# Turning attention probabilities ahead of the outputs of the pair in front, in the first block of a two-block forward pass

## The chip, the cores and the metric

The kernel runs on one core of one Trainium2 chip. Its time is the device time of one execution in microseconds (us). TensorE (PE) does matmuls and transposes, VectorE (DVE) and ScalarE (ACT) do everything that works on whole tiles, GpSimd (POOL) adds up norms, and SyncE (SP) issues the weight loads.

## The reference, cut to what matters

Two transformer blocks run one after the other on 256 tokens of width 1024, in float32. The first block has two layers (`DEPTH = 2`), and takes 256 context tokens along. Each of its layers mixes tokens in three ways (attention, an mLSTM and a pooling mixer), projects the result (`w_out`) and has a SwiGLU. The change touches the attention of these two layers alone:

```python
def block_attention(q, k, v):          # 8 query heads, 2 key heads, head size 64
    ...
    def one_block(qi):                 # 128 queries
        s = jnp.einsum('bqhgd,bkhd->bhgqk', qi, k, preferred_element_type=F32) * scale
        p = jax.nn.softmax(s, -1).astype(v.dtype)
        return jnp.einsum('bhgqk,bkhd->bqhgd', p, v)

# hybrid_layer
    att_l = block_attention(q_l, jnp.concatenate([k_l, k_c], 1), jnp.concatenate([v_l, v_c], 1))
    ...
    xl = xl + g1_l * (jnp.concatenate([att_l, ml_l, pool_l], -1) @ w_out)
    if with_ctx_out:                   # layer 0 only
        att_c = block_attention(q_c, k_c, v_c)
```

A block of 128 latent queries of one head meets 512 keys, a block of 128 context queries meets 256.

## The kernel before, in words

Every engine has its own instruction stream, written out by hand, and waits on semaphores for the others. The attention of a layer is split into units: one head of one block of 128 queries. Two units, one for each key head, make a pair. Layer 0 has 32 units in 16 pairs: 8 pairs with 512 keys, then 8 with 256. Layer 1 has 16 units in 8 pairs, all with 512 keys. I write S(i) for the scores of pair i, T(x) for the turning (transposing) of unit x, and O(i) for the outputs of pair i; pair i is the units 2i and 2i+1.

- PE (`pe_attention`), at step i: S(i) into PSUM (line 1328, semaphore `at_s`), then O(i-2), the product of values and turned probabilities (line 1342, `at_o`), then T(2i-2) and T(2i-1) (line 1353, `at_t`). O(i-2) waits until both turned units of its pair have been copied out of PSUM (`at_pt`). T(x) waits until unit x's probabilities are normalised (`at_p`), and until the PSUM bank that it shares with unit x-2 has been copied out (`at_pt`). At step 1, the readout of the mLSTM is turned as well (line 1607).
- DVE (`dve_attention`), at step j: the row maximum of unit j (line 1394, needs S), its scaling (1395, `at_max`), the reciprocal of the sum of unit j-1 (1400), the normalising of unit j-1 (1402, `at_p`), and at every second step the low half of an output (1411, `at_out`). At steps 3 and 5, pieces of the mLSTM readout are in it (1807, 1814), and at step 8 the split of a weight tile (580).
- ACT (`act_attention`), at step j: the exponentials of unit j (1370, `at_exp`), the copy of turned unit j-2 out of PSUM (1378, `at_pt`), and at every second step the high half of the output of a pair three in front (1383). At step 8, it also has the split of a weight tile (571).

A weight tile of the projections is split into a high and a low part: ACT writes the high one (571), DVE the rest (580). The projection behind the attention (`pe_residual`, lines 600 to 602 for each of its three products) needs the attention's last output. SP loads weights into a ring of buffers (line 553), two of its transfers start while the two attentions run; none is issued from PE.

Of the kernel before, what the change touches and what calls it, by code (L numbers as in the profile page):

```python
# [12 lines left out]
P = 128  # L13
# [419 lines left out]
def build(nc, dram, out):  # L433
    ctx = ExitStack()
    with ctx:
# [3 lines left out]
        def sem(name):  # L439
            return ctx.enter_context(nc.semaphore(name))  # L440
# [58 lines left out]
        ps = ctx.enter_context(nc.psum_tensor("ps", [P, 8, 512], F32))  # L499

        def K(name):
            at, n = CONST_AT[name]
            return const[:, at:at + n]
# [788 lines left out]
        def dve_keys(dve, layer):  # L1292
# [6 lines left out]
        at_s, at_max, at_exp, at_p, at_t, at_pt, at_o, at_high, at_out = (  # L1299
            sem(f"at_{x}") for x in ("scores", "max", "exp", "probs", "turned", "probsT", "o", "high", "out"))  # L1300

        def attention_units(layer):


            turns = [(2, 3), (0, 1)] if layer < DEPTH - 1 else [(2, 3)]
            return [(qt, j, b, (2 if qt < 2 else 4) * P) for turn in turns for j in range(4) for qt in turn for b in range(2)]
# [3 lines left out]
        def score_bank(x):  # L1310
            return 2 + x % 4

        def pe_attention(pe, layer):


            units, base = attention_units(layer), AT_BASE[layer]
            n = len(units) // 2
            pe.wait_ge(qk_k, layer + 1)
            pe.wait_ge(ml_h, 4 * layer + 4)
            for i in range(n + 2):  # L1320
                if i == 1:
                    pe.wait_ge(pl_low, layer + 1)
                if i < n:
                    if i >= 2:
                        pe.wait_ge(at_exp, base + 2 * i - 2)
                    for x in (2 * i, 2 * i + 1):
                        qt, j, b, nk = units[x]
                        pe.matmul(ps[:, score_bank(x), 0:nk], proj[64 * b:64 * b + 64, AQ + j, qt * P:(qt + 1) * P],
                                  proj[64 * b:64 * b + 64, AK, 0:nk], start=True, stop=True).then_inc(at_s, 1)
                if i == 1:  # L1330
                    pe_readout(pe, layer)
                if i >= 2:
                    p = i - 2
                    nk = units[2 * p][3]
                    pe.wait_ge(at_pt, base + 2 * p + 2)
                    if p == 0:
                        pe.wait_ge(ml_mixed, layer + 1)
                    if p >= 2:
                        pe.wait_ge(at_out, base // 2 + p - 1)
                    for s in range(nk // P):  # L1340
                        for b in range(2):
                            mm = pe.matmul(ps[64 * b:64 * b + 64, p % 2, 0:P], tm[:, s, AV + 64 * b:AV + 64 * b + 64],  # L1342
                                           probsT[(2 * p + b) % 4][:, s * P:(s + 1) * P], start=(s == 0), stop=(s == nk // P - 1),
                                           skip_group_check=True)
                            if s == nk // P - 1:
                                mm.then_inc(at_o, 1)
                if 1 <= i <= n:
                    for x in (2 * i - 2, 2 * i - 1):
                        pe.wait_ge(at_p, base + x + 1)
                        if x >= 2:  # L1350
                            pe.wait_ge(at_pt, base + x - 1)
                        for s in range(units[x][3] // P):
                            mm = pe.transpose(ps[:, 6 + x % 2, s * P:(s + 1) * P], probs[x % 4][:, s * P:(s + 1) * P], K("ident"))
                        mm.then_inc(at_t, 1)
            pe.wait_ge(at_out, base // 2 + n)

        def act_attention(act, layer):
# [132 lines left out]
        probs = [ebuf[:, b, d] for b in range(2) for d in range(2)]  # L1490
# [20 lines left out]
        def ml_tiles(layer):  # L1511
            return range(0, 4) if layer < DEPTH - 1 else range(2, 4)
# [90 lines left out]
        def pe_readout(pe, layer):  # L1603
            pe.wait_ge(ml_hn, layer + 1)
            for tt in ml_tiles(layer):
                for f in range(2):
                    mm = pe.transpose(ps[:, f, tt * P:(tt + 1) * P],
                                      hsum[:, tt, 2 * f:2 * f + 2, :].rearrange("p h v -> p (h v)"), K("ident"))
            mm.then_inc(ml_hT, 1)
# [1231 lines left out]
        @block.tensor  # L2841
        def _(pe):
            pe_ada(pe)
            for layer in range(DEPTH):
                c0, n = unit_tokens(layer, False)
                pe_project(pe, layer)
                pe_mlstm(pe, layer)
                pe_attention(pe, layer)
                pe_residual(pe, f"out{layer}", mix, c0, n, KT, norm=2 * layer + 1, order=OUT_ORDER)
                pe_ffn(pe, layer, 2 * layer + 1, 2 * layer + 2)  # L2850
            pe_ffn(pe, 2, 5, 6)
            pe_qkv(pe)
            pe_second(pe)
            pe_rwkv(pe)
            pe_merge(pe)
            pe_residual(pe, "w_o", merged, 0, T, KT, norm=7)
            pe_ffn(pe, 3, 7, 8)
# [220 lines left out]
```

## Time and profile before

| | us |
|---|---|
| runs (three) | 2003.0, 2010.8, 2010.97; median 2010.8 |
| the profiled execution, its own time | 2009.54 |
| its span, first to last instruction | 2007.7 |
| attention of layer 0, S(0) to the projection | 62.7 (222.76 to 285.48) |
| attention of layer 1, S(0) to the projection | 40.7 (875.52 to 916.21) |

The profile gives, for one execution, when each instruction started and how long it took, and for each idle stretch what ended it. Its page says that PE is busy for 1865.1 us of the span, DVE for 1134.5 and ACT for 757.2, and that the mean granted TensorE clock is 0.968 of full speed. Starts are in microseconds from the first instruction. A matmul's end is modelled, so its length holds some time in which the next one is already under way: the distance between two starts is what one costs its successor.

### The profile page before, as it was taken

To read this page: it belongs to the slowest core of one execution; us is meant where nothing else is said; L and a number is where in the kernel's file an instruction comes from. 1 tells how busy PE (TensorE), PEld (TensorE's weight loads), DVE (VectorE), ACT (ScalarE), POOL (GpSimd) and SP (SyncE) were. 2 spreads that over 40 slices of the span, in tenths; PEclk is the share of its full clock that TensorE was granted. 3 is DMA by queue.
4 is the path that set the end of the run, shared out by engine and by line. 5 is a ranking of instruction groups with operands and counts; after the bars stand their busy time and mean duration, and the time that the engine had idled before them with its cause. 6 is when DMAs were issued, how large, how long until landed. Compare 5 with 4: busy or idle time off the path is not lost.

```text
span 2007.7 us, 34066 instructions
## 1 busy us (share of the span) xinstructions
PE 1865.1 (93%) x14848; PEld 1632.5 (81%) x14848; DVE 1134.5 (57%) x1692; ACT 757.2 (38%) x1054; POOL 307.7 (15%) x270
## 2 busy tenths in 40 slices
PE   6999888999999979988999999999998999889998
PEld 3777555877888768857999999989987777789997
DVE  2644565554353338566555576556765666566654
ACT  3432563221122225355333443343454333344332
POOL 1011001999080010100000100002001111000000
PEclk8999999999999988898999999999999999999999
DMA  8154112565353222203555555544340111255552
GB/s 339 64 191 183 68 43 84 182 211 173 121 186 123 85 74 72 76 22 105 185 177 184 200 189 177 176 144 165 128 158 23 44 44 44 77 173 174 188 173 80
DMA packets 39605, 266.20 MB, mean 133 GB/s; under 512 B 4384, under 2 KB 4512, under 8 KB 11168
## 3 DMA queue, kind: packets, MB, share of 16 engines
q1 hardware_dynamic: 34560, 244.10, 35.2%
q0 software_dynamic: 4608, 16.78, 2.7%
q8 instruction: 117, 1.92, 0.4%
q10 hardware_dynamic: 288, 3.15, 0.4%
q14 instruction: 32, 0.26, 0.0%
HBM read 262.96 MB, written 1.05 MB: 131 GB/s over the span
## 4 chain that ended last, share of the span: by engine, by line
PE 78%; DVE 9%; POOL 5%; ACT 5%; issue 2%; DMA 1%; SPq 0%; ACTq 0%; DVEq 0%; POOLq 0%
PE ps L600 19%; PE ps L601 18%; PE ps L602 18%; PE ps L2751 3%; POOL work L1015 2%; DVE W L580 2%; PE ps L926 1%; PE ps L606 1%; PE ps L1555 1%; POOL work L1016 1%; PE ps L608 1%; PE ps L607 1%; PE ps L1342 1%; DMA ring<-w_ada_dram 1%; PE ps L2297 1%
## 5 line engine op out<-in xcount | busy, mean ns | idle before, releaser
L580 DVE TENSOR_TENSOR W<-ring,W 128x2048 fp32r<-128x2048 f32 (+2 forms) x194 | 439.5, 2267 | 260.6 <-ACT W L571 260.3
L571 ACT ACTIVATE W<-ring 128x2048 fp32r<-128x2048 f32 (+2 forms) x194 | 359.0, 1853 | 136.0 <-PE ps L602 129.0
L600 PE MATMUL ps<-h_lat,W 128*128 128x256 f32 x1056 | 301.9, 286 | 4.0 <-DVE h_lat L747 4.0
L601 PE MATMUL ps<-h_lat,W 128*128 128x256 f32 x1056 | 300.0, 284 | 0.0
L602 PE MATMUL ps<-h_lat,W 128*128 128x256 f32 x1056 | 299.9, 284 | 0.0
L600 PEld LDWEIGHTS ps<-h_lat,W 128*128 128x128 f32 x1056 | 203.6, 193 | 5.5 <-issue 4.6
L601 PEld LDWEIGHTS ps<-h_lat,W 128*128 128x128 f32 x1056 | 204.0, 193 | 0.3 <-issue 0.2
L602 PEld LDWEIGHTS ps<-h_lat,W 128*128 128x128 f32 x1056 | 203.9, 193 | 0.0
L699 POOL TENSOR_TENSOR work<-work 128x512 f32<-128x512 f32 (+1 forms) x48 | 48.7, 1014 | 997.4 <-ACT work L681 806.9
L600 PE MATMUL ps<-hidden_lat,W 128*128 128x256 f32 x528 | 150.4, 285 | 6.3 <-DVE hidden_lat L912 6.3
L601 PE MATMUL ps<-hidden_lat,W 128*128 128x256 f32 x528 | 150.2, 284 | 0.0
L602 PE MATMUL ps<-hidden_lat,W 128*128 128x256 f32 x528 | 150.1, 284 | 0.0
L909 DVE TENSOR_TENSOR work<-work,ps 128x256 f32<-128x256 f32 (+1 forms) x88 | 42.9, 488 | 189.3 <-ACT work L884 189.2
L600 PE MATMUL ps<-h_both,W 128*128 128x512 f32 x352 | 140.6, 399 | 9.0 <-DVE h_both L747 9.0
L601 PE MATMUL ps<-h_both,W 128*128 128x512 f32 x352 | 137.7, 391 | 0.0
L602 PE MATMUL ps<-h_both,W 128*128 128x512 f32 x352 | 137.6, 391 | 0.0
L884 ACT ACTIVATE work<-ps 128x512 f32<-128x512 f32 (+1 forms) x44 | 21.6, 491 | 267.7 <-PE ps L602 267.7
L600 PEld LDWEIGHTS ps<-hidden_lat,W 128*128 128x128 f32 x528 | 102.1, 193 | 6.9 <-DVE hidden_lat L912 6.9
L602 PEld LDWEIGHTS ps<-hidden_lat,W 128*128 128x128 f32 x528 | 102.1, 193 | 0.0
L601 PEld LDWEIGHTS ps<-hidden_lat,W 128*128 128x128 f32 x528 | 102.0, 193 | 0.0
L681 ACT ACTIVATE work<-xT 128x256 f32<-128x256 f32 (+1 forms) x64 | 31.5, 497 | 173.6 <-DVE xT L645 115.0
L600 PE MATMUL ps<-h_mix,W 128*128 128x256 f32 x312 | 93.3, 299 | 3.9 <-DVE h_mix L745 3.9
(387 smaller groups left out, 4207.0 us busy)
## 6 DMA issues: line engine op xcount, KB each, us to landing
ring<-w_up_dram SPq DMA_DIRECT2D x88, 1024.0 KB, 5.0
ring<-w_down_dram SPq DMA_DIRECT2D x43, 1024.0 KB, 4.9
ring<-w_ada_dram SPq DMA_DIRECT2D x32, 1024.0 KB, 6.0
work<-w_ada_dram POOLq DMA_DIRECT2D x32, 512.0 KB, 4.3
ring<-w_rkv_dram SPq DMA_DIRECT2D x13, 1024.0 KB, 5.0
ring<-w_fm_dram SPq DMA_DIRECT2D x10, 1024.0 KB, 4.9
ring<-w_out_dram SPq DMA_DIRECT2D x8, 1024.0 KB, 4.9
ring<-w_gates_dram SPq DMA_DIRECT2D x8, 1024.0 KB, 4.9
```

What stands on the lines that cost most here:

```text
L571: act.activation(slots[SLOT[s]][:, 0, 0:cols], ring[:, u % RING, 0:cols], ACT.Copy).then_inc(w_high, 1)
L580: dve.tensor_tensor(slots[SLOT[s]][:, 1, 0:cols], ring[:, u % RING, 0:cols], slots[SLOT[s]][:, 0, 0:cols], ALU.subtract).then_inc(w_low, 1)
L600: pe.matmul(o, slots[SLOT[s]][:, 0, at:at + cols], high, start=first, stop=False)
L601: pe.matmul(o, slots[SLOT[s]][:, 0, at:at + cols], low, start=False, stop=False)
L602: return pe.matmul(o, slots[SLOT[s]][:, 1, at:at + cols], high, start=False, stop=final)
L606: pe.matmul(o, high, slots[SLOT[s]][:, 0, at:at + cols], start=first, stop=False)
L681: ins = act.activation(square[:, at, 0:n], xT[:, m, c0:c0 + n], ACT.Square, scale=1.0 / 32)
L699: pool.tensor_tensor(square[:, 0, 0:n], square[:, 0, 0:n], square[:, square_at(m), 0:n], ALU.add).then_inc(norm_add, 1)
L884: act.activation(stage_buf[:, i % 2, 0:n], gate, ACT.Silu).then_inc(act_emptied, 1)
L909: dve.tensor_tensor(t, t, up_banks(g, n)[1], ALU.mult).then_inc(dve_emptied, 1)
L1015: plink(pool.tensor_tensor(half, half, c, ALU.mult))
L2751: mm = pe.matmul(ps[:, 3, m * T:(m + 1) * T], ring[:, u % RING, x * P:(x + 1) * P], h2[:, k, :], start=(k == 0), stop=(k == KT - 1))
```

## The change

In the PE stream of `pe_attention` alone, the block that turns T(2i-2) and T(2i-1) is moved ahead of the block that makes O(i-2). The order at step i was S(i), O(i-2), T(2i-2), T(2i-1); it becomes S(i), T(2i-2), T(2i-1), O(i-2). Every wait stays with the instruction that it belonged to. The streams of ACT, DVE, POOL and SP are the same, and so is the arithmetic. Both layers of the first block run through this code.

```diff
                 if i == 1:
                     pe_readout(pe, layer)
+                if 1 <= i <= n:
+                    for x in (2 * i - 2, 2 * i - 1):
+                        pe.wait_ge(at_p, base + x + 1)
+                        if x >= 2:
+                            pe.wait_ge(at_pt, base + x - 1)
+                        for s in range(units[x][3] // P):
+                            mm = pe.transpose(ps[:, 6 + x % 2, s * P:(s + 1) * P], probs[x % 4][:, s * P:(s + 1) * P], K("ident"))
+                        mm.then_inc(at_t, 1)
                 if i >= 2:
                     p = i - 2
                     nk = units[2 * p][3]
...
                             if s == nk // P - 1:
                                 mm.then_inc(at_o, 1)
-                if 1 <= i <= n:
-                    for x in (2 * i - 2, 2 * i - 1):
-                        pe.wait_ge(at_p, base + x + 1)
-                        if x >= 2:
-                            pe.wait_ge(at_pt, base + x - 1)
-                        for s in range(units[x][3] // P):
-                            mm = pe.transpose(ps[:, 6 + x % 2, s * P:(s + 1) * P], probs[x % 4][:, s * P:(s + 1) * P], K("ident"))
-                        mm.then_inc(at_t, 1)
             pe.wait_ge(at_out, base // 2 + n)
```

## Rows read from the trace of the kernel before

**Rows 1.** Page, part 4: the chain that ended last, shares of the span by engine.

```profile
PE 78%; DVE 9%; POOL 5%; ACT 5%; issue 2%; DMA 1%; SPq 0%; ACTq 0%; DVEq 0%; POOLq 0%
```

**Rows 2.** Timeline, one 512-key step: start, length, engine, line, operation, count, [idle before].

```profile
250.86 1.13 PE L1328 MATMUL ps<-work 64*128 64x512 f32 x4
...
252.02 0.69 DVE L1394 TENSOR_REDUCE work<-ps 128x1 f32<-128x512 f32 x1 [0.40 <-PE ps L1328]
252.59 1.09 PE L1342 MATMUL ps<-work 128*64 128x128 f32 x16 [0.61 <-ACT work L1378]
...
253.06 0.49 DVE L1402 TENSOR_SCALAR work<-work 128x512 f32<-128x512 f32 x1
...
253.62 1.09 PE L1353 MATMUL ps<-const,work 128*128 128x128 f32 x8
...
254.31 0.60 ACT L1378 ACTIVATE work<-ps 128x512 f32<-128x512 f32 x1 [0.45 <-PE ps L1353]
...
254.64 1.13 PE L1328 MATMUL ps<-work 64*128 64x512 f32 x4
...
254.96 0.78 ACT L1370 ACTIVATE work<-ps,work 128x512 f32<-128x512 f32 x1
...
255.72 0.61 ACT L1378 ACTIVATE work<-ps 128x512 f32<-128x512 f32 x1
...
256.38 1.09 PE L1342 MATMUL ps<-work 128*64 128x128 f32 x16 [0.61 <-ACT work L1378]
```

**Rows 3.** Timeline, one 256-key step.

```profile
265.34 0.70 PE L1328 MATMUL ps<-work 64*128 64x256 f32 x4
...
266.07 0.42 DVE L1394 TENSOR_REDUCE work<-ps 128x1 f32<-128x256 f32 x1
...
266.65 0.66 PE L1342 MATMUL ps<-work 128*64 128x128 f32 x8 [0.61 <-ACT work L1378]
...
266.85 0.35 DVE L1402 TENSOR_SCALAR work<-work 128x256 f32<-128x256 f32 x1
...
267.24 0.65 PE L1353 MATMUL ps<-const,work 128*128 128x128 f32 x4
...
267.71 0.38 ACT L1378 ACTIVATE work<-ps 128x256 f32<-128x256 f32 x1 [0.28 <-PE ps L1353]
...
267.83 0.70 PE L1328 MATMUL ps<-work 64*128 64x256 f32 x4
```

**Rows 4.** Timeline around the split of a weight tile, layer 0.

```profile
245.03 0.49 DVE L1402 TENSOR_SCALAR work<-work 128x512 f32<-128x512 f32 x1
...
245.58 0.76 PE L1353 MATMUL ps<-const,work 128*128 128x128 f32 x4 [3.89 <-DVE work L1402]
...
246.27 2.08 PE L1328 MATMUL ps<-work 64*128 64x512 f32 x4
```

**Rows 5.** Timeline, ends of the attention of layer 0 and of layer 1.

```profile
277.78 0.70 PE L1328 MATMUL ps<-work 64*128 64x256 f32 x4
...
281.49 0.35 DVE L1402 TENSOR_SCALAR work<-work 128x256 f32<-128x256 f32 x1
...
283.67 1.12 PE L1342 MATMUL ps<-work 128*64 128x128 f32 x8 [0.84 <-DVE mix L1411]
...
905.84 1.13 PE L1328 MATMUL ps<-work 64*128 64x512 f32 x4
...
911.05 0.49 DVE L1402 TENSOR_SCALAR work<-work 128x512 f32<-128x512 f32 x1
...
914.38 1.09 PE L1342 MATMUL ps<-work 128*64 128x128 f32 x16 [0.91 <-ACT work L1378]
```

**Rows 6.** Windows: stretch, its us, busy us of each engine, granted clock, DMA share, GB/s.

```profile
277.78:285.48 7.70, 4.32 (x37) 2.72 (x36) 4.35 (x17) 4.94 (x18) 0.00 (x0) 0.87 0.00 1
285.50:290.40 4.90, 4.90 (x12) 3.84 (x13) 3.46 (x2) 3.20 (x2) 0.00 (x0) 0.50 0.19 25
290.40:295.30 4.90, 4.90 (x23) 4.04 (x22) 1.91 (x3) 0.63 (x1) 0.00 (x0) 1.00 0.86 348
```

## Prediction, made before the change was run

> **What bounds the kernel now.** The chain that ended last comes first: 78% of it is PE [rows 1], so whatever delays PE on this chain is paid in full. The two attentions last 62.7 and 40.7 us, 103 of 2008, so what the change can move is small. Within them the question is what closes one step of the loop, and the timeline of one step answers it.
>
> With 512 keys, one step takes 3.78 us from S to S (250.86 to 254.64). PE waits in one place: O starts at 252.59 after 0.61 idle, released by ACT's copy L1378 [rows 2]. Follow that loop: O start to T start 1.03 (252.59 to 253.62); T start to ACT's first copy 0.69 (to 254.31, and ACT had idled 0.45 for it); then the small high half and the exponentials, 0.65 to 254.96; exponentials to the second copy 0.76 (255.72); its 0.61 and a 0.05 hand-over to the next O at 256.38. Sum: 1.03 + 0.69 + 0.65 + 0.76 + 0.66 = 3.79, the step. So O, T and ACT bound it, and DVE's work lies beside O. With 256 keys the step is 2.49 (265.34 to 267.83), with O again behind 0.61 of idle released by the same copy [rows 3].
>
> **The change, part by part.** Nothing is added or taken away: O and T keep their counts and lengths. Two things happen.
>
> Removed: O (1.03) no longer stands between S and T, so ACT's copy of the first unit can come earlier and the loop above is cut. That much looks like a gain.
>
> Moved in front: T(2i-1) needs the probabilities of unit 2i-1, and DVE normalises these only behind the maximum of unit 2i, which needs S(i). In the trace this cannot be overtaken: the maximum starts at 252.02 after 0.40 idle, released by S, 1.16 after S's start; then 1.04 over scaling and reciprocal to the normalising (253.06), and 0.49 for it [rows 2]. Before, O filled PE during this. After, PE has only T(2i-2), whose probabilities are there, and then stands in front of T(2i-1), with O(i-2) and S(i+1) queued behind the wait. DVE and ACT wait for that S(i+1) in turn. The new loop, S to S, with 512 keys:
>
> - S to maximum 1.16, maximum to normalising 1.04, normalising 0.49 and hand-over 0.06 (245.03 + 0.49 to T at 245.58) [rows 2, 4]: T(2i-1) starts 2.75 behind S.
> - T(2i-1), four transposes and the change to the next group: 0.59 (267.24 to 267.83) [rows 3].
> - O: 1.03 [rows 2]. Sum 2.75 + 0.59 + 1.03 = 4.37, against 3.79: **0.58 longer**.
>
> With 256 keys: S to maximum 0.73, maximum to normalising 0.78 (266.07 to 266.85), 0.35 and 0.05, so T(2i-1) at 1.91. Its two transposes: four take 0.59 and eight take 1.02, so one takes 0.11, and two take 0.37. O, eight matmuls, 0.59 (266.65 to 267.24). Sum 2.87 against 2.49: **0.38 longer** [rows 2, 3].
>
> The maximum's 0.73 with 256 keys could be less, as DVE was not idle there; it is bounded below by S's own length, 0.70 [rows 3]. The hand-over I bound by 0.02 and 0.08. Neither moves the sum by over 0.5 us in all. That O behind T could start quicker, its weights loaded during the wait, could give back at most what O shows as change of group beyond its matmuls (1.03 - 8 x 0.11 = 0.15) in some 18 steps, 2.7 us at the most; below nothing I see no reason. I take no such gain, since a wait ahead of O in the trace leaves its 1.03 as it is [rows 2].
>
> Now the count. **Layer 0**: by the first weight split S has moved little. By walking the order forward with the terms above, S(3) comes 0.95 later (the first outputs, 1.03, lay under DVE's readout before, and now follow it) and S(4) 0.4 more; but the split stalls everyone (PE idle 3.89 until T(7) at 245.58) [rows 4] and takes most of that. What gets past is the later T(5), 0.33, which ACT's stream carries into the split, and O(2), 1.03, which ran before the stall and now stands behind it: S(5) comes 1.35 later. Three steps of 0.58 follow (S(5) to S(8)): 3.1 in all. The two steps at the change to 256 keys have terms of both kinds and give -0.1 and +0.2. Five steps of 0.38 (S(10) to S(15)): 5.1. ****Its end** gains: the last T no longer stands behind an O that waits. Before, unit 31's probabilities were ready 4.06 behind S(15) (281.49 + 0.35 - 277.78); 0.28 of that was ACT waiting for a T that now comes early, so T(31) starts at 4.06 - 0.28 + 0.05 = 3.8. Its copy begins 0.47 later and takes 0.38, 0.05 to hand over: last O at 4.7, where it was 5.9 (283.67) [rows 3, 5]; 1.1 is given back. Sum +4.0 us.: T(31) needs only its probabilities, 3.74 behind S(15) by ACT's and DVE's rows, and the last O follows at 3.74 + 0.47 + 0.44 + 0.05 = 4.70. Before it was 5.85; so 1.1 is given back. Sum +4.0 us.
>
> **Layer 1**: S(5) 1.6 later by the same steps, two steps of 0.58 to S(7), 2.8. At its end, unit 15's probabilities were ready 5.70 behind S(7) (911.05 + 0.49 - 905.84); without ACT's wait of 0.45 for T, T(15) starts at 5.3, and 0.59 and 1.03 later comes the last O, at 6.9, against 8.54 (905.84 to 914.38) [rows 2, 5]: 1.7 back. Sum +1.1 us.
>
> Both: **+5.1 us**. Behind either attention the projection waits for the last output, so the 5.1 goes through in full. No DMA is issued by PE; SP's load during the split moves by less than 1 us. Made against the profiled execution's own time, 2009.54 + 5.1 = 2014.6; that execution lies 1.3 under the median of the runs, 2010.8, from which the same sum gives 2015.9; between the two I forecast 2015.
>
> **The clock.** At the end of layer 0 PE is busy 4.32 of 7.70 us, and afterwards the projection starts at granted clock 0.50, the 1.2 GHz level: 12 matmuls in 4.90 us, where the next 4.90 us at full clock hold 23 [rows 6]. That costs 11/23 x 4.9 = 2.3 us. A shorter end may save that, and a loop with 0.6 us more idle may bring such a fall elsewhere. The Trainium skill's page "TensorE: Matmul & The Clock Gate", section "What's actually happening", says that the throttled state is the default and activity lifts it. It speaks against this change, which makes PE idler in each step; the trace agrees as far as its falls follow idle stretches.
>
> **The rivals.**
>
> *The gate takes the loop (slower by over 0.5%).* S took 2.08 in place of 1.13 in the one step at 1.2 GHz [rows 4]. In the new loop S, T(2i-1) and O are all in the chain: some 0.95 + 0.45 + 0.9 = 2.3 more in each 512-key step, 1.3 in each 256-key step. It decides from the point where the new idle in a step (PE busy about 3.2 of 4.37, where it was 3.2 of 3.78) makes the clock fall; in all 10 and 8 steps that is 33 us, 2048; in a quarter of them 8 us, 2023. For it: the fall at the end of layer 0, with busy 4.32 of 7.70 = 0.56. Against: busy stays near 0.7.
>
> *The end gains the clock.* The sum, less the 2.3: 2012.
>
> *ACT's loop was all (faster).* If T(2i-1) found its probabilities ready, the step would fall to DVE's own work, about 3.15 with 512 keys (3.78 less DVE's 0.40 idle and the wait for ACT ahead of its low half, some 0.2), 0.6 less in 12 steps and next to nothing with 256 keys, and the ends' 2.8: -10 us, 2000. For it: PE's only steady wait is ACT's. Against: the maximum of 2i stands ahead of the normalising of 2i-1 in DVE's stream.
>
> *It doesn't do what it says.* If PE could let O pass the waiting T, nothing would be lost, 2010. By the same page, section "Step-by-step: what each phase is for", matmuls stay in program order. The trace shows the same: T and S never start while O waits [rows 2].
>
> **How the numbers follow.** Forecast 0.66; the end gains the clock 0.14; nothing changes 0.06; faster 0.05; gate 0.09. The three runs of before spread over 8 us (2003.0 to 2010.97), which no row explains, and widens each case: the range goes from 2006 to 2022, which leaves out most of the faster case and of the gate. A difference of 0.5% (10 us, under 2000.7 or over 2020.9) is about what can be told from none: faster 0.04 (half of its case, and scatter), slower 0.13 (the gate and scatter of the forecast), no difference 0.83.
>
> **What would show it.** Right: S to S 4.37 and 2.87 in steady steps; T(2i-1) alone behind idle time released by DVE L1402, some 1.0 us per 512-key step; O without idle ahead of it; ACT's copy no longer waiting for T(2i-2); last O to the projection as before, at 6.9 behind layer 1's last S. Wrong: steps at or under 3.78 with idle still released by ACT; a granted clock of 0.50 within the steady steps; or the attentions' lengths as forecast (66.7 and 41.8 us) and the total not.

## The result

| | before | changed |
|---|---|---|
| median of 20 runs each | 2010.32 us (2003.0 to 2015.17) | 2017.86 us (2011.6 to 2025.18) |
| ratio, 95% interval | 1 | 1.004, 1.0029 to 1.005 |
| span of the profiled execution | 2007.7 | 2016.8 |
| attention of layer 0, S(0) to the projection | 62.72 | 67.81 |
| attention of layer 1 | 40.68 | 42.55 |
| the 512-key step, S to S | 3.78 | 4.36 |
| the 256-key step | 2.49 | 2.88 |

The change makes the kernel slower by 0.4%, 6 to 10 us. In the two profiles, the attentions account for 5.1 + 1.9 = 7.0 us of a span that is 9.0 longer. The ratio isn't the quotient of the two medians, and the two can be some us apart where the times lie in groups; below, each difference says which it is taken from. One execution of the kernel before, in the last group of runs, took 2648.13 us at a granted clock of 0.65, and is left out.

The timeline of the changed kernel, a 512-key step (start, length, engine, line; [idle before it <- what ended it]); it answers to [rows 2]. T is line 1338 now, O is line 1350.

```profile
254.64 1.13 PE L1328 MATMUL ps<-work 64*128 64x512 f32 x4
...
255.70 0.66 PE L1338 MATMUL ps<-const,work 128*128 128x128 f32 x4
255.80 0.69 DVE L1394 TENSOR_REDUCE work<-ps 128x1 f32<-128x512 f32 x1 [1.19 <-PE ps L1328]
...
256.85 0.49 DVE L1402 TENSOR_SCALAR work<-work 128x512 f32<-128x512 f32 x1
...
257.39 0.66 PE L1338 MATMUL ps<-const,work 128*128 128x128 f32 x4 [1.03 <-DVE work L1402]
...
257.55 0.58 ACT L1378 ACTIVATE work<-ps 128x512 f32<-128x512 f32 x1
...
257.98 1.09 PE L1350 MATMUL ps<-work 128*64 128x128 f32 x16
...
259.00 0.70 PE L1328 MATMUL ps<-work 64*128 64x512 f32 x2
```

Read it as a ring. S starts at 254.64; the maximum of unit 2i follows 1.16 later, and DVE had been idle 1.19 for it, where that was 0.40. The normalising of unit 2i-1 starts 1.05 behind the maximum, and 0.54 after its start T(2i-1) begins: PE idled 1.03 for it. O and the next S have no wait of their own left, they only come 0.59 and 1.02 behind. Sum 1.16 + 1.05 + 0.54 + 0.59 + 1.02 = 4.36. The 256-key step, which answers to [rows 3], is the same ring with shorter pieces:

```profile
273.21 0.70 PE L1328 MATMUL ps<-work 64*128 64x256 f32 x4
...
274.72 0.35 DVE L1402 TENSOR_SCALAR work<-work 128x256 f32<-128x256 f32 x1
...
275.13 0.44 PE L1338 MATMUL ps<-const,work 128*128 128x128 f32 x2 [0.85 <-DVE work L1402]
...
275.49 0.66 PE L1350 MATMUL ps<-work 128*64 128x128 f32 x8
...
276.08 0.49 PE L1328 MATMUL ps<-work 64*128 64x256 f32 x2
```

PE's waits in the attention of layer 0, summed by who ended them (total, times, longest). The same view of the kernel before has 8.9 us in 13 waits of O for ACT's copy, and 5.0 in 3 of T for DVE. One wait has taken the place of the other, and is larger.

```profile
PE ps L1338 <- DVE work L1402: 17.5, 15, 4.5
PE ps L1328 <- DVE mix L1461: 1.8, 1, 1.8
```

The weight split, which answers to [rows 4]:

```profile
247.04 0.66 PE L1338 MATMUL ps<-const,work 128*128 128x128 f32 x4 [4.47 <-DVE work L1402]
247.63 1.96 PE L1350 MATMUL ps<-work 128*64 128x128 f32 x16
249.51 1.90 PE L1328 MATMUL ps<-work 64*128 64x512 f32 x4
```

Here O, 1.09 long elsewhere, is 1.96, and S 1.90 in place of 1.13. The windows view (us, busy of each engine, granted clock) shows the clock at 0.51, the 1.2 GHz level, in just this stretch, behind 4.47 us of idle PE. The second and third row answer to [rows 6]: the end of layer 0's attention, 7.00 us where it was 7.70, and the first 4.9 us of the projection.

```profile
247.63:251.10 3.47, 3.47 (x21) 2.06 (x20) 0.96 (x4) 1.59 (x5) 0.00 (x0) 0.51 0.60 248
284.71:291.71 7.00, 5.03 (x38) 3.10 (x36) 3.85 (x16) 4.37 (x16) 0.00 (x0) 0.78 0.01 4
291.70:296.60 4.90, 4.89 (x14) 3.90 (x15) 3.44 (x2) 3.23 (x2) 0.00 (x0) 0.62 0.12 13
```

### The profile page after: what moved, and what is told of

Same layout as the page of the kernel before. It is cut to its first block, busy times and chain, and to the rows that moved or that the text cites. A ratio compares the mean times of both kernels' runs of the same rounds, so it can differ in the third digit from the quotient of the medians.

```text
span 2016.8 us, 34066 instructions
## 1 busy us (share of the span) xinstructions
PE 1873.8 (93%) x14848; PEld 1637.0 (81%) x14848; DVE 1133.5 (56%) x1692; ACT 756.4 (38%) x1054; POOL 307.4 (15%) x270
## 3 DMA queue, kind: packets, MB, share of 16 engines
HBM read 262.96 MB, written 1.05 MB: 131 GB/s over the span
## 4 chain that ended last, share of the span: by engine, by line
PE 80%; DVE 9%; POOL 4%; ACT 3%; issue 2%; DMA 1%; SPq 0%; DVEq 0%; ACTq 0%; POOLq 0%
PE ps L600 19%; PE ps L601 19%; PE ps L602 19%; PE ps L2751 3%; POOL work L1015 2%; PE ps L926 1%; DVE W L580 1%; PE ps L1555 1%; PE ps L606 1%; PE ps L607 1%; PE ps L608 1%; PE ps L1350 1%; POOL work L1016 1%; DMA ring<-w_ada_dram 1%; PE ps L2297 1%
```

## The experiments

The theory at this point: T(2i-1) needs a normalising that stands behind a maximum that needs S(i), and O, once beside that chain, now stands in it, ahead of S(i+1). Rivals: clock falls in any place, the move as such, or the wait of T(2i-1) alone. All ratios below are to the kernel before on the same chip. The comments in the cuts of code are added here.

### One layer alone

Layer 0 alone, against the changed kernel; layer 1 alone has the two numbers exchanged.

```diff
-                if 1 <= i <= n:
+                if layer == 0 and 1 <= i <= n:     # the turns ahead of O(i-2)
...
+                if layer == 1 and 1 <= i <= n:     # the turns behind O(i-2)
```

> The new order in layer 0 alone, the old one in layer 1. Theory (the step is closed by S, DVE's normalising, T(2i-1), O): layer 0 shows what the changed kernel shows, S to S 4.36 and 2.88, attention about 67.5 us, where it was 62.7, and layer 1 stays at 40.7; the time is 4 to 5 us over before (ratio 1.0020 to 1.0025). Rival (the measured loss is mostly clock falls that the changed order brings anywhere): the ratio need not split by layers, and could be all of 1.004 or none.

> The new order in layer 1 alone. Theory: attention of layer 1 about 42.5 us where it was 40.7, layer 0 at 62.7; 1 to 2 us over before (ratio 1.0005 to 1.001), so that this and the kernel with layer 0 alone add up to the whole change. Rival: 3 us or more over before with layer 1's attention still at 42.5, the rest in clock falls elsewhere.

Layer 0 alone: 1.0028 (1.0012 to 1.0044), attentions 67.85 and 41.23 us, steps 4.36 and 2.88. Layer 1 alone: 1.002 (1.0006 to 1.0035), attentions 62.53 and 42.44. Each layer shows the lengths of the whole change where the new order is, and nearly those of before where it isn't (41.23 against 40.68: its step with the split was 8.35 long, where 7.89 was). The ratios add up to 1.0048, against 1.004. Layer 1's 4 us by the ratio (2.9 by the medians) are above the 1 to 2 that were expected, and are what the rival named (3 or more with that attention still at 42.5); the interval, 1 to 7 us, excludes neither. So the attentions' lengths split as the theory says; the time of so small a part can't decide between the two.

### The first turn alone ahead of O

T(2i-2) goes ahead of O(i-2), T(2i-1) stays behind it. The cut is against the kernel before.

```diff
+                if 1 <= i <= n:
+                    for x in (2 * i - 2,):
...
                 if i >= 2:
                     p = i - 2
...
                 if 1 <= i <= n:
-                    for x in (2 * i - 2, 2 * i - 1):
+                    for x in (2 * i - 1,):
```

> Half of the change: T(2i-2) goes ahead of O(i-2), T(2i-1) stays behind it. Theory: only the turn that has to wait for DVE's normalising does the harm, and the other one, ahead, lets ACT copy it earlier. O then fills PE while DVE normalises. Walking the order forward with the terms of the trace, a 512-key step takes 3.33 (3.78 before) and a 256-key step 2.35 (2.49); layer 0 ends 4.1 and layer 1 2.3 us earlier: 6 us under before (ratio 0.997). Rival (any move of turns ahead of outputs costs, since outputs then stand behind a copy or a bank that is not free): steps at or over 3.78 and the time at or over before.

Measured 0.9957 (0.9941 to 0.9973), median 1999.72 us: faster than before. The timeline of one of its 512-key steps (T(2i-2) is line 1338, O 1350, T(2i-1) 1361) has PE without a wait that the view shows:

```profile
251.75 1.13 PE L1328 MATMUL ps<-work 64*128 64x512 f32 x4
252.81 0.66 PE L1338 MATMUL ps<-const,work 128*128 128x128 f32 x4
253.39 1.09 PE L1350 MATMUL ps<-work 128*64 128x128 f32 x16
254.50 0.65 PE L1361 MATMUL ps<-const,work 128*128 128x128 f32 x4
255.08 1.13 PE L1328 MATMUL ps<-work 64*128 64x512 f32 x4
```

3.33 from S to S, as walked, and 2.29 with 256 keys (2.35 walked). T(2i-1) starts 2.75 behind S here too (251.75 to 254.50): that is DVE's distance, unchanged, but O lies beside it. The rival that any turn ahead of O costs has fallen. The attentions are 4.2 us shorter than before (59.67 and 39.56), less than the 4.1 + 2.3 expected: around the split, S(4) to S(6) lasts 8.26 + 5.70 in layer 0, where it was 7.91 + 4.59. The time gained is 10.6 us by the medians and 8.6 by the ratio (5 to 12), so more than the attentions show, while the 6 expected aren't excluded.

### The scores ahead of O

The whole change, and S(i+1) goes between T(2i-1) and O(i-2). The cut is against the changed kernel.

```diff
-                if i < n:
-                    if i >= 2:
-                        pe.wait_ge(at_exp, base + 2 * i - 2)
+                if i < 2:
...
+                if 1 <= i < n - 1:                  # behind the turns, ahead of O(i-2)
+                    pe.wait_ge(at_exp, base + 2 * i)
+                    for x in (2 * i + 2, 2 * i + 3):
```

> The whole change, and S(i+1) is issued behind T(2i-1) but ahead of O(i-2). Theory: what made the changed kernel slow is that S(i+1), and with it DVE, stands behind O; with O out of that loop the step is S, DVE's normalising, T(2i-1): 4.37 less 1.03, 3.33, and 2.35 with 256 keys. 7.5 us under before (ratio 0.9963), although T(2i-1) still waits for DVE. Rival (the wait of T(2i-1) for DVE is itself the loss, wherever O stands): steps near 4.36 stay, and the time is some 5 us over before.

Measured 0.9977 (0.9966 to 0.9988), attentions 59.18 and 38.28 us, steps 3.33 and 2.29. The step is 1.03 shorter than in the changed kernel, the length of O. A 512-key step (S is line 1342, O 1354, T 1336):

```profile
257.88 1.13 PE L1342 MATMUL ps<-work 64*128 64x512 f32 x4
258.94 1.09 PE L1354 MATMUL ps<-work 128*64 128x128 f32 x16
259.97 1.32 PE L1336 MATMUL ps<-const,work 128*128 128x128 f32 x8
261.22 1.13 PE L1342 MATMUL ps<-work 64*128 64x512 f32 x4
```

T(2i-1) loads its weights at 260.63, again 2.75 behind S, but O lies in this distance, and PE has no wait that the view shows. With 256 keys 0.26 us of wait are left in each step. The view of PE's waits in layer 0 still has 10 for DVE, but 8.0 of its 9.3 us lie at the start, the split and the end:

```profile
PE ps L1336 <- DVE work L1406: 9.3, 10, 4.6
```

So the rival that steps stay near 4.36 wherever O stands has fallen: what costs is that S(i+1), which feeds DVE, stands behind O, which stands behind the wait. Not shown is a step in which the wait stays and costs nothing. Written out, the order here is S(i+1), O(i-2), T(2i), T(2i+1): the order of the kernel before, with the outputs one pair further back, whose inputs have long been copied. The 0.61 us of idle in front of O [rows 2] are gone, which is why it beats before; it isn't the changed order with a repair.

The time is 4.6 us under before by the ratio (2 to 7) and 7.2 by the medians, where 7.5 were expected. The profiled execution, 2006.42, lies 3.3 over the median; its first attention begins at 227.99 where the others begin near 222.7, behind a clock fall at 158 us, in code that is the same in all kernels.

### The normalising ahead of the maximum

The changed kernel, and DVE does the normalising of unit 2i-1 before the maximum of unit 2i.

```diff
+                if 1 <= i <= n and i % 2 == 0:      # ahead of the maximum of unit i
+                    x = i - 1
+                    dve.wait_ge(at_exp, base + x + 1)
...
-                if 1 <= i <= n:
+                if 1 <= i <= n and i % 2 == 1:
```

> The changed kernel, and DVE normalises unit 2i-1 ahead of the maximum of unit 2i, at every second step. Theory: T(2i-1) waited because this normalising stood behind a maximum that needs S(i). Taking it out of the way frees T(2i-1) from S(i); the step then closes through ACT's exponentials: walked forward, 3.86 with 512 keys (4.36 in the changed kernel) and 2.83 with 256 (2.88), 2.1 us under the changed kernel, 3 over before. Rival (T(2i-1) waits for something else, such as the exponentials alone): steps stay 4.36, and the time too.

Measured 1.0021 (1.0008 to 1.0033), 4.2 us over before by the ratio where 3 were expected. The 512-key steps are 3.70 to 3.88 and the 256-key steps 2.84 to 2.85, as walked; the attentions 66.33 and 41.24 us, 2.8 less than in the changed kernel. PE's wait ahead of T(2i-1) falls from 1.03 to 0.38 and 0.56 (timeline, T line 1338):

```profile
255.41 0.66 PE L1338 MATMUL ps<-const,work 128*128 128x128 f32 x4 [0.38 <-DVE work L1396]
...
259.30 0.66 PE L1338 MATMUL ps<-const,work 128*128 128x128 f32 x4 [0.56 <-DVE work L1396]
```

So the maximum that needs S(i) is in the ring. With 512 keys nearly all of the 0.58 comes back (steps 0.48 to 0.66 shorter), with 256 keys only 0.03 of 0.39: DVE now waits for ACT's exponentials ahead of this normalising (0.47 and 0.24 idle), which close the next ring. The step with the split is longer than in the changed kernel, 9.53 and 9.71 for 8.66 and 9.14.

### Extra turns during the split

36 transposes of the identity into the bank that T(7) overwrites, between the two waits of T(7). Put into the changed kernel and into the one before. The two waits change places ahead of every turn, which is a second difference.

```diff
                     for x in (2 * i - 2, 2 * i - 1):
-                        pe.wait_ge(at_p, base + x + 1)
                         if x >= 2:
                             pe.wait_ge(at_pt, base + x - 1)
+                        if x == 7:
+                            for _ in range(36):
+                                pe.transpose(ps[:, 7, 0:P], K("ident"), K("ident"))
+                        pe.wait_ge(at_p, base + x + 1)
```

> The changed kernel, and while PE waits for the weight split (4.47 us idle ahead of T(7)) it turns the identity 36 times into bank 7, which T(7) overwrites: about 3.9 us of extra matmuls in idle time. Theory: what the changed kernel lost over the walk (1.9 us in the two attentions) is the low clock behind this wait, which now meets O as well as S. Without it, S(4) to S(5) and S(5) to S(6) go from 8.66 and 5.13 to 7.8 and 4.36 in layer 0, from 9.14 and 5.10 to 7.8 and 4.36 in layer 1; the attentions last about 66.2 and 40.5, and the time is some 3.7 us under the changed kernel, 4 over before. Rival (the split's wait itself is longer in the new order): the steps stay over 8.5.

> The kernel before with the same 36 extra turns in the same wait. Theory: here only S and what follows in one step ran at the low clock, S(5) to S(6) 4.59 and 4.84 where a step is 3.78, so 1.9 us come back: ratio 0.999. Against this kernel the changed one with extra turns is 5.1 us slower, the walk's sum without any clock term. Rival: the low clock costs both orders the same, so that the two with extra turns differ by the same 6.9 us (in the two attentions) as the two without.

Changed kernel with extra turns: 1.0006 (0.9993 to 1.0019). Its timeline at the split:

```profile
242.78 4.09 PE L1338 MATMUL ps<-const 128*128 128x128 f32 x36
247.35 0.66 PE L1341 MATMUL ps<-const,work 128*128 128x128 f32 x4 [0.48 <-DVE work L1405]
247.94 1.09 PE L1353 MATMUL ps<-work 128*64 128x128 f32 x16
```

O is back at 1.09. S(4) to S(5) and S(5) to S(6) are 7.74 and 4.42 in layer 0 (8.66 and 5.13 in the changed kernel), 7.75 and 4.42 in layer 1 (9.14 and 5.10). The rival, a longer wait for the split, has fallen: it was the low clock behind it. Layer 1's attention lasts 40.74, as expected (40.5). Layer 0's, 67.23, is 1 over its 66.2: a clock fall came earlier, at 235 us, behind 1.98 us of idle PE, and steps S(2) to S(4) were 5.56 and 5.37 long. A plain miss is the steady step, 4.42 and 2.94, 0.06 more each; the exchanged waits are the only difference in these steps.

The kernel before with extra turns: 0.9983 (0.9971 to 0.9994), S(4) to S(5) and S(5) to S(6) 7.75 and 3.70 in layer 0, attentions 61.27 and 39.55, 2.6 us less where 1.9 were expected; 0.5 of it is the end of layer 0, which had no clock fall here. Its steady steps stay at 3.78 and 2.49, so the exchanged waits cost nothing where PE has idle time in front of O.

The rival was that the two orders with extra turns still differ by 6.9 us in the attentions. They do differ by 7.2, so the sum doesn't speak for the theory. Layer by layer: in layer 1, where no clock fall disturbs either, they differ by 40.74 - 39.55 = 1.19 us, against 1.1 walked and 1.87 without extra turns. In layer 0 they differ by 5.96; the fall at 235 us, which stands ahead of the extra turns, made two steps 1.3 longer, and the exchanged waits cost some 0.7, which leaves 3.9 against 4.0 walked. This is a subtraction, and no run shows layer 0 of the changed kernel at full clock throughout. Going by the ratios, each good to some 2.5 us either way, the two kernels differ by 4.6 us, which can't part 5.1 from 6.9.

### A version that beats both, and repeats

The first turn ahead of O, both turns ahead in the last step, and the extra turns. The cut is against the kernel with the first turn alone ahead, and leaves the extra turns out.

```diff
+                if i == n and 1 <= i <= n:          # T(2i-1) ahead of O(i-2), last step only
...
-                if 1 <= i <= n:
+                if i < n and 1 <= i <= n:
```

> A version that should beat both: T(2i-2) ahead of O(i-2), T(2i-1) behind it, except in the last step, where both go ahead, and the 36 extra turns in the wait for the split. Theory: steps of 3.33 and 2.29 as with the first turn alone; the ends 0.3 to 0.7 shorter each, as where both turns went ahead of O; S(4) to S(5) and S(5) to S(6) down from 8.26 and 5.70 (5.23 in layer 1) to about 7.8 and 3.4. Together some 6 us under the kernel with the first turn alone: 1994, ratio 0.993. Rival: the extra turns only move the clock's fall to another wait, and nothing is gained over 1999.7.

Measured 0.9958 (0.9943 to 0.9974), attentions 57.02 and 36.66 us, steps 3.40 and 2.35, ends 6.08 and 8.50. The attentions are 5.5 us shorter than with the first turn alone, but the median, 2004.25, misses the expected 1994: four executions lie at 1995.4 to 1999.0, five at 2004.3 to 2006.2. Three kernels ran once more, side by side, and the last one also without its extra turns:

> The changed kernel once more, beside the next three on one chip. Theory: attentions 67.8 and 42.5 us again, steps 4.36 and 2.88, ratio to before 1.004; the stretch between the two attentions and the one behind them within 2 us of before's 590.0 and 1091.5, either way. Rival (the change lengthens the rest of the kernel too): both stretches longer than before's again and by 2 us or more together.

> The first turn alone ahead, once more. Its median was 10.6 us under before, where its attentions are 4.2 us shorter. Theory: the other 6 us were clock falls elsewhere that one chip spared it; a second measurement gives 4 to 8 us under before. Rival: 10 us again, so that shifting the rest of the kernel in time has a lasting worth of its own.

> The first turn ahead of O, both in the last step, no extra turns. Theory: ends shorter by 0.3 and 0.7 than with the first turn alone (6.08 and 8.5), the attentions 59.4 and 38.9, the time 1 us under it. Rival: the last T waits for DVE ahead of O and nothing is gained.

> The version with 36 extra turns once more. Its attentions were 57.0 and 36.7, 9.7 us shorter than before's, but its median only 6.7 us under before, with runs at 1996 to 1999 and at 2004 to 2006. Theory: the attention's gain is real and the upper group lost it to a clock fall outside; again 6 to 10 us under before, in two groups. Rival: the extra turns cost elsewhere, and it is always behind the same version without them.

| | median, us | ratio, 95% interval | attentions, us | S(0) at | between the attentions | behind them |
|---|---|---|---|---|---|---|
| before | 2010.86 | 1 | 62.7, 40.7 | 222.8 | 590.0 | 1091.5 |
| changed | 2017.12 | 1.0036 (1.0022 to 1.0049) | 66.8, 42.5 | 221.9 | 586.1 | 1092.6 |
| first turn ahead | 2000.41 | 0.9953 (0.9941 to 0.9965) | 58.7, 39.4 | 222.7 | 587.7 | 1089.4 |
| the same, both turns in the last step | 2003.76 | 0.9972 (0.9961 to 0.9984) | 58.0, 38.9 | 228.7 | 586.9 | 1094.1 |
| the same, with extra turns | 1998.58 | 0.9943 (0.9928 to 0.9958) | 57.0, 36.7 | 228.7 | 588.2 | 1091.9 |

The changed kernel repeats its loss, so it is firm. The rival, that it lengthens the rest too, finds nothing here: the stretches between and behind are 3.9 shorter and 1.0 longer than those of before, whose row holds the profile shown ahead of the prediction; the 3.9 are outside the 2 us that were expected. This profile had the case "the end gains the clock": its attention of layer 0 ended in 6.08 us, and the projection started at full clock.

```profile
286.83 1.20 PE L1350 MATMUL ps<-work 128*64 128x128 f32 x16
288.76 0.50 PE L600 MATMUL ps<-mix,W 128*128 128x512 f32 x1 [0.73 <-DVE mix L1411]
289.57 0.39 PE L600 MATMUL ps<-mix,W 128*128 128x512 f32 x1
```

Nonetheless its median is 6.3 over before. The profiled execution, 2011.71, is the lowest of its eight, so this case needn't be the typical one.

The first turn ahead gained again, 9.5 us by the ratio (7 to 12) and 10.5 by the medians, where 4 to 8 were expected; 10 was the rival's figure, and the interval doesn't exclude the upper end of the other. Its profiles show where it comes from. The attentions give 4.2 and 5.3 us; both outer stretches, which the attention's code doesn't touch, are 1.5 to 2.3 us shorter than before's each, and have 8 and 12 us less at the 1.2 GHz level in all. One such place, first of the kernel before, then of the kernel with the first turn ahead, the same code with the same 2.3 us of idle PE in it:

```profile
1268.00:1273.40 5.40, 3.11 (x27) 2.91 (x26) 3.52 (x6) 2.22 (x2) 0.00 (x0) 1.00 0.50 171
1273.40:1276.80 3.40, 3.40 (x19) 3.40 (x18) 1.88 (x1) 0.00 (x0) 0.00 (x0) 0.50 0.28 65
```

```profile
1261.00:1266.00 5.00, 2.71 (x22) 2.51 (x22) 3.32 (x5) 2.05 (x2) 0.00 (x0) 1.00 0.50 154
1266.00:1271.40 5.40, 5.40 (x48) 5.40 (x47) 2.29 (x1) 0.17 (x1) 0.00 (x0) 1.00 0.51 167
```

Why the clock falls there in one and not in the other stays open, and so does whether a kernel can count on it.

The version with extra turns was expected 6 to 10 under before, in two groups, and came 11.5 under by the ratio: four executions at 1995.6 to 1999.3, two at 2004.2 and 2004.7. Its rival, that it is always behind the same version without them (2003.76), has fallen. One profile of each group is at hand, 1997.23 and 2004.19: their attentions are equal, and S(0) comes 4.7 us later in the second and the stretch behind is 2.8 longer, so that the upper group's loss lies outside the attention.

Both turns in the last step shorten the ends as expected (6.08 and 8.50), and the time doesn't follow. In three profiles S(0) comes near 228 (the scores ahead of O and the last two rows of the table); each has 13.7 us at the 1.2 GHz level from 158 or 159 us on, though PE was busy throughout. The windows from 155 to 175 us, first of the kernel with both turns in the last step, then of the kernel before:

```profile
155.00:175.00 20.00, 20.00 (x97) 16.11 (x95) 5.05 (x13) 2.24 (x5) 0.92 (x2) 0.66 0.41 145
```

```profile
155.00:175.00 20.00, 20.00 (x139) 15.01 (x141) 8.71 (x23) 4.05 (x10) 1.79 (x4) 1.00 0.55 198
```

When it comes, none of the code in which these kernels differ has run; it costs some 5 to 6 us and is of the size of the effects measured here.

## Why the prediction was right or wrong

- **The ring that closes a step: right.** Forecast 4.37 and 2.87, measured 4.36 and 2.88. T(2i-1) was forecast 2.75 behind S and came 2.75 (254.64 to 257.39). The wait that it names, 1.0 us for DVE L1402, is there with 1.03, and O has no idle ahead of it, nor has ACT's copy (257.55). Two of its members were taken out one at a time: O (scores ahead, 3.33) and the maximum (3.7 to 3.9).
- **What the prediction left unsaid: half of the change is a gain.** It called the cut of ACT's loop a gain and let the wait outweigh it, without asking whether the two turns can part.
- **The count up to the split: right where the clock was full, short where it wasn't.** In layer 0, S(3) came 0.90 and S(4) 1.35 later, for 0.95 and 1.35. Layer 1 with extra turns has S(5) 1.63 later, for 1.6, and its attention 1.19 longer, for 1.1. In the profile of the change itself S(5) came 2.09 later in layer 0 and 2.90 in layer 1, for a forecast of 1.35 and 1.6. The mis-sized term is the low clock behind the split. The prediction had seen it act on S [rows 4] and priced O at that clock at 0.9 more, but only in the rival of a gate that takes the whole loop. In the forecast itself O moved from ahead of the wait to behind it at full speed. It took 1.96 us and 1.98, where it takes 1.09; in layer 1 T(7) was slow too, 1.12 for 0.66. Behind S(6), the steps differ from before's as forecast. That the low clock is the term is shown for layer 1; in layer 0 it rests on the subtraction above. It is most of the difference between 5.1 and the 7.0 of the attentions.
- **The ends: right in kind.** 8.54 was to shrink by 1.7 in layer 1; S(7) to the projection shrank by 1.87 (10.37 to 8.50). Layer 0 gave 0.70 back, for 1.1: its last O ran at the low clock (7.00 in all). At full clock in both orders, the two kernels with extra turns, it is 7.24 and 6.14, the forecast 1.1. The prediction works T(31) out twice, as 3.8 and as 3.74 behind S(15); it came 3.78 behind (284.71 to 288.49). No row is given for the 3.74 and its 0.44, but both ways lead to the same end.
- **The gate as a rival.** No steady step of the changed kernel ran at the low clock, in either of its profiles, with PE's 1.03 us of idle in each.
- **The total: in the range, under the mark.** 2015 was forecast and 2017.86 measured; the forecast change is 5.1, the measured 7.5 (6 to 10 by the ratio). Some 2 us of the rest are the term above. What is left isn't larger than the interval, and the second profile, with attentions 5.9 longer than before's for the first one's 7.0, shows how much of such a figure one clock fall moves.
- The page "TensorE: Matmul & The Clock Gate" of the Trainium skill, section "What's actually happening", was weighed as a rule against this change: the throttled state is the default. Here that held in one way only: the step's own 1.03 us of idle did nothing, and the 4.47 us were followed by the low level, which is what made the moved O dear. The falls don't all follow idle time, though: three profiles have one from 158 or 159 us on, with PE busy 20.00 of 20.00 us around it.

## What to carry to other kernels

When two instructions of an in-order engine change places, write down the ring of waits that each of them is in before and after: an instruction that filled a wait for free becomes part of the chain once it stands behind that wait, ahead of the one that feeds the other engines. Move only the part whose inputs are there; here that turned 0.4% of loss into 0.4 to 0.5% of gain, of which the attentions account for 0.2 to 0.3%. And price what is moved behind a long idle stretch at the clock that the trace shows there, since it will be what runs first.

## What the runs showed of the hardware

- Behind 4.47 us of idle TensorE the clock was at the 1.2 GHz level and O took 1.96 us for 1.09. 36 throw-away transposes (4.09 us) in that wait kept it at full in each of the four profiles that have them, and S(4) to S(6) became 1.63 and 2.07 us shorter in the changed kernel.
- Two semaphore waits in exchanged order ahead of the same transposes came with steps 0.06 us longer where PE sets the pace or stands in the ring (4.36 to 4.42, 3.33 to 3.40), and with none where it has 0.61 us of idle (3.78 in both). It was not tested apart from the extra turns, of which these steps have none.
- The same 2.3 us of idle in the same code were followed by a clock fall in the kernel before (1273.40, 3.40 us at 0.50) and not in the one with the first turn ahead.
- Clock falls come in stretches with TensorE busy throughout as well (13.7 us from 158 or 159 us on, in three of fourteen profiles), and cost 5 to 6 us there. What brings them is open.
